# Two MLPs with the up-projection turned round: weights held, 256 tokens streamed, and the second norm applied to the sum

## The reference, cut to what matters

```
h2 = rms_norm(x, norm2_w) * (1 + scale2) + shift2
x  = x + gate2 * (square(relu(h2 @ w_ff1)) @ w_ff2)          # first MLP

h  = rms_norm_2(x, norm_mlp_g)
x  = x + square(relu(h @ mlp_w_in)) @ mlp_w_out              # second MLP
```

## Time and profile before

| | |
|---|---|
| median of the runs | 2431.68 us |
| the two runs | 2431.48 and 2431.89 us |
| span of the profiled execution | 2431.4 us |
| PE busy | 2359.0 us (97%) |
| VectorE busy | 1594.6 us (66%) |
| ScalarE busy | 1039.6 us (43%) |

### The profile page before, as it was taken

How to read it: one execution, slowest core, us unless ns; L and a number is a source line. 1 busy time by engine, 2 the same in 40 slices (tenths; PEclk the granted TensorE clock), 3 DMA queues, 4 the chain that set the end, 5 groups by cost and what they waited for, 6 DMA issues and landing times.

```text
span 2431.4 us, 27934 instructions
## 1 busy us (share of the span) xinstructions
PE 2359.0 (97%) x10954; PEld 1968.0 (81%) x10954; DVE 1594.6 (66%) x1284; ACT 1039.6 (43%) x890; POOL 51.4 (2%) x56
## 2 busy tenths in 40 slices
PE   4899999999999999999999999999999999999999
PEld 3777888887888888888887888878888888888887
DVE  7868989987666666655568456556555565565554
ACT  2245553435333333333334556664443433433432
POOL 1011000001000000000000000000000000000000
PEclk9789999999999999999999999999999999999999
DMA  9988987755676776655554545444555655555552
GB/s 355 362 300 311 361 311 268 252 199 169 231 241 231 234 242 224 224 190 181 183 190 171 177 160 168 156 138 158 183 191 183 191 184 192 189 188 190 190 189 104
DMA packets 235129, 520.30 MB, mean 214 GB/s; under 512 B 9705, under 2 KB 10162, under 8 KB 232370
## 3 DMA queue, kind: packets, MB, share of 16 engines
q1 hardware_dynamic: 234352, 519.15, 63.2%
q10 hardware_dynamic: 706, 0.17, 0.0%
HBM read 517.19 MB, written 2.10 MB: 214 GB/s over the span
## 4 chain that ended last, share of the span: by engine, by line
PE 90%; DVE 4%; DMA 2%; ACT 2%; issue 1%; DVEq 1%; POOL 1%; ACTq 0%; SPq 0%
PE PS L257 28%; PE PS L259 28%; PE PS L258 28%; DMA ada_raw<-in_w_ada_dram 2%; PE PS L1695 2%; PE PS L1734 1%; PE PS L1669 1%; DVE w_lo L247 1%; PE PS L306 1%; ACT w_hi L243 1%; POOL rstd L609 1%; PE PS L1679 1%; DVE ada_acc L1144 0%; DVEq L1511 0%; PE PS L1799 0%
## 5 line engine op out<-in xcount | busy, mean ns | idle before, releaser
L247 DVE TENSOR_TENSOR w_lo<-raw,w_hi 128x2048 fp32r<-128x2048 f32 x392 | 897.6, 2291 | 688.4 <-ACT w_hi L243 683.4
L243 ACT ACTIVATE w_hi<-raw 128x2048 fp32r<-128x2048 f32 x392 | 750.9, 1916 | 1149.1 <-PE PS L259 1137.7
L257 PE MATMUL PS<-w_hi,A_hi 128*128 128x512 f32 x2112 | 839.7, 398 | 10.0 <-DVE A_lo L361 3.5
L259 PE MATMUL PS<-w_hi,A_lo 128*128 128x512 f32 x2112 | 827.5, 392 | 0.0
L258 PE MATMUL PS<-w_lo,A_hi 128*128 128x512 f32 x2112 | 827.2, 392 | 0.0
L257 PEld LDWEIGHTS PS<-w_hi,A_hi 128*128 128x128 f32 x2112 | 400.6, 190 | 92.2 <-ACT qT L738 2.8
L259 PEld LDWEIGHTS PS<-w_hi,A_lo 128*128 128x128 f32 x2112 | 399.5, 189 | 84.9
L258 PEld LDWEIGHTS PS<-w_lo,A_hi 128*128 128x128 f32 x2112 | 400.4, 190 | 81.2 <-issue 1.0
L257 PE MATMUL PS<-w_hi,H_hi 128*128 128x512 f32 x1024 | 401.6, 392 | 2.0 <-issue 1.3
L259 PE MATMUL PS<-w_hi,H_lo 128*128 128x512 f32 x1024 | 398.9, 390 | 0.0
L258 PE MATMUL PS<-w_lo,H_hi 128*128 128x512 f32 x1024 | 398.5, 389 | 0.0
(11 more groups left out here) (267 smaller groups left out, 1108.0 us busy)
## 6 DMA issues: line engine op xcount, KB each, us to landing
raw<-in_w_ff_dram SPq DMA_DIRECT2D x128, 1024.0 KB, 5.3
raw<-in_mlp_w_in_dram SPq DMA_DIRECT2D x64, 1024.0 KB, 5.4
raw<-in_mlp_w_out_dram SPq DMA_DIRECT2D x64, 1024.0 KB, 5.0
raw<-in_w_in_dram SPq DMA_DIRECT2D x56, 1024.0 KB, 8.1
X<-in_w_ada_dram SPq DMA_DIRECT2D x96, 512.0 KB, 5.7
raw<-in_sb_w_qkv_dram SPq DMA_DIRECT2D x48, 1024.0 KB, 5.1
ada_raw<-in_w_ada_dram SPq DMA_DIRECT2D x32, 1024.0 KB, 9.8
raw<-in_w_out_dram SPq DMA_DIRECT2D x16, 1024.0 KB, 6.6
```

The source lines that it names most:

```text
L243: act.activation(w_hi[:, j, :, :], raw[:, j, :, :], ACT.Copy).then_inc(hi_rdy, 1)
L247: dve.tensor_tensor(w_lo[:, j, :, :], raw[:, j, :, :], w_hi[:, j, :, :].bitcast(F32), ALU.subtract).then_inc(lo_rdy, 1)
L257: pe.matmul(bank(pair + t), h, w_hi[:, j, k, :], start=first, stop=False)
L259: mm = pe.matmul(bank(pair + t), l, w_hi[:, j, k, :], start=False, stop=last)
```

## The change

- PE: all up-projections but the first unit of the first MLP use the new `up_chunk`. It holds 128 x 128 blocks of the weights (`w_hi`, `w_lo`) as the stationary operand and streams the 256 tokens of `A_hi` or `A_lo`. A chunk has 4 column blocks x 4 k tiles x 3 = 48 matmuls of 256 columns. The result has hidden features on partitions and tokens along the row, four pieces of 256 in two banks.
- The turn is gone for these units: ScalarE makes relu into `RE` and, after a drain, `Square` of `RE` straight into `H_hi`; VectorE squares `RE` into `SQ` and makes `H_lo` as `SQ - H_hi` (`rest`). The first unit of the first MLP keeps its turn.
- The next up on PE waits for `relu_rdy` instead of `sq_rdy`.
- Second MLP: relu has no scale and doesn't wait for the norm. The sum is gathered in `ACC` (its first down copies, `fresh`), `row_r` is `rstd` squared, and after the loop VectorE adds `ACC * row_r` to `X` in eight steps of 512 columns; the last down block is added in two such steps per quarter, with the same factor.

```diff
+        def up_chunk(pe, B, j, pair):
+            pe.wait_ge(lo_rdy, 4 * B + j + 1)
+            for c in range(CH):
+                out = bank(pair + c // 2, S * (c % 2), S * (c % 2) + S)
+                cols = slice(P * c, P * c + P)
+                for k in range(CH):
+                    h, l = A_hi[:, CH * j + k, :], A_lo[:, CH * j + k, :]
+                    first = j == 0 and k == 0 and c % 2 == 0
+                    last = j == CH - 1 and k == CH - 1 and c % 2 == 1
+                    pe.matmul(out, w_hi[:, j, k, cols], h, start=first, stop=False)
+                    pe.matmul(out, w_hi[:, j, k, cols], l, start=False, stop=False)
+                    mm = pe.matmul(out, w_lo[:, j, k, cols], h, start=False, stop=last)
+            mm.then_inc(chunk_done, 1)
...
 # ScalarE
-                def relu(B, U, pair):
+                def relu(B, U, pair, par):
                     act.wait_ge(chunk_done, 4 * (B + 1))
                     if not isinstance(U, int) or U:
                         act.wait_ge(sq_rdy, U)
-                    if m == 0:
-                        act.activation(RE[:, :, :], PS[:, pair:pair + 2, :], ACT.Relu).then_inc(relu_rdy, 1)
-                    else:
-                        for t in range(T):
-                            ins = act.activation(RE[:, t, :], bank(pair + t), ACT.Relu, scale=rstd[:, t:t + 1])
-                        ins.then_inc(relu_rdy, 1)
...
+                        if not isinstance(U, int) or U > 1:
+                            act.wait_ge(h_hi, U)
+                    act.activation(RE[:, :, :], PS[:, pair:pair + 2, :], ACT.Relu).then_inc(relu_rdy, 1)
+                    if par is not None:
+                        act.drain()
+                        act.activation(H_hi[:, par, :, :].rearrange("p k s -> p (k s)"), REf, ACT.Square).then_inc(h_hi, 1)
...
 # VectorE
-                    other = RE[:, :, :] if m else PS[:, pair:pair + 2, :]
-                    dve.tensor_tensor(SQ[:, :, :], other, RE[:, :, :], ALU.mult).then_inc(sq_rdy, 1)
+                        dve.wait_ge(h_lo, U)
+                    dve.tensor_tensor(SQ[:, :, :], RE[:, :, :], RE[:, :, :], ALU.mult).then_inc(sq_rdy, 1)
...
+                        if fresh:
+                            dve.wait_ge(chunk_done, 4 * B + j + 1)
+                            dve.tensor_copy(ac, PS[:, b:b + 2, :]).then_inc(acc_read, 1)
...
+                    d()
+                    for b in range(4):
+                        for t in range(T):
+                            xs = X[:, t, NC_ * b:NC_ * (b + 1)]
+                            dve.scalar_tensor_tensor(out=xs, in0=ACC[:, t, NC_ * b:NC_ * (b + 1)], scalar=row_r[:, t:t + 1], in1=xs,
+                                                     op0=ALU.mult, op1=ALU.add)
+                    d()
...
-                dve.tensor_tensor(X[:, :, cols], X[:, :, cols], PS[:, pb:pb + 2, :], ALU.add).then_inc(acc_read, 1)
+                for t in range(T):
+                    ins = dve.scalar_tensor_tensor(out=X[:, t, cols], in0=bank(pb + t), scalar=row_r[:, t:t + 1], in1=X[:, t, cols],
+                                                   op0=ALU.mult, op1=ALU.add)
+                ins.then_inc(acc_read, 1)
...
 # PE
                     if turned is None and not turn_last:
-                        pe.wait_ge(sq_rdy, U)
+                        pe.wait_ge(relu_rdy, U)
                     for j in range(CH):
-                        a_chunk(pe, B, j, pair, turned)
+                        if turned is not None:
+                            pe.wait_ge(a_lo, KT // 2 * turned + 2 * (j + 1))
+                        up_chunk(pe, B, j, pair)
...
-                        if j == 1 and turn_next:
-                            turn_unit(U + 1)
```

More of the change, by code:

```diff
@@ L859, in up @@
+                    act.activation(RE[:, :, :], PS[:, pair:pair + 2, :], ACT.Relu).then_inc(relu_rdy, 1)
+                    if par is not None:
+                        act.drain()
+                        act.activation(H_hi[:, par, :, :].rearrange("p k s -> p (k s)"), REf, ACT.Square).then_inc(h_hi, 1)
+                def up(B, U, par):
                     for j in range(CH):
                         split_hi(act, B + 1, j)
[L861 to L866, removed]
@@ L868, in down @@
-                def down(B, U, par, end=False):
+                    relu(B, U, 0, par)
+                def down(B):
                     for j in range(CH):
[L870 to L873, removed]
+                        split_hi(act, B + 1, j)
                 for j in range(CH):
                     split_hi(act, M + 1, j)
-                if m:
-                    act.wait_ge(rstd_rdy, POWER_OF[5])
@@ L879, in mlp @@
-                relu(M, NU * m, pairs[2])
+                relu(M, NU * m, pairs[2], 0 if m else None)
                 for j in range(CH):
                     split_hi(act, M + 2, j)
[L882 to L885, removed]
+                    if m == 0 and j == 1:
+                        act.wait_ge(h_tr, 1)
+                        act.activation(H_hi[:, 0, :, :].rearrange("p k s -> p (k s)"), PS[:, 6:8, :], ACT.Copy).then_inc(h_hi, 1)
@@ L886, in mlp @@
+                relu(M + 1, NU * m + 1, 0, 1)
+                down(M + 2)
                 with act.Fori(0, NU // 2 - 1) as i:
                     for e in range(2):
-                        up(M + 3 + 4 * i + 2 * e, NU * m + 2 + 2 * i + e)
-                        down(M + 4 + 4 * i + 2 * e, NU * m + 1 + 2 * i + e, e)
+                        up(M + 3 + 4 * i + 2 * e, NU * m + 2 + 2 * i + e, e)
+                        down(M + 4 + 4 * i + 2 * e)
             act.wait_ge(g_rdy, 5)
@@ L1461, in rows_half, with mlp, square @@
                 d()
-            def mlp(m, M, total):
-                def square(U, pair):
+            def mlp(m, M):
+                def square(U):
                     dve.wait_ge(relu_rdy, U + 1)
+                    if isinstance(U, int) and U == 1:
+                        dve.wait_ge(h_tr, 1)
                     if not isinstance(U, int) or U:
-                        dve.wait_ge(h_tr, U)
-                    other = RE[:, :, :] if m else PS[:, pair:pair + 2, :]
-                    dve.tensor_tensor(SQ[:, :, :], other, RE[:, :, :], ALU.mult).then_inc(sq_rdy, 1)
+                        dve.wait_ge(h_lo, U)
+                    dve.tensor_tensor(SQ[:, :, :], RE[:, :, :], RE[:, :, :], ALU.mult).then_inc(sq_rdy, 1)
                 def gate_sum(pair, half):
@@ L1484, in up, with rest @@
                             gate_sum(pair, 0)
-                    square(U, 0)
-                def turn(U, par):
+                    square(U)
+                def rest(U, par, turned=False):
                     dve.wait_ge(h_hi, U + 1)
-                    flat = "p k s -> p (k s)"
-                    dve.tensor_tensor(H_lo[:, par, :, :].rearrange(flat), PS[:, 6:8, :],
-                                      H_hi[:, par, :, :].rearrange(flat).bitcast(F32), ALU.subtract).then_inc(h_lo, 1)
+                    dve.wait_ge(sq_rdy, U + 1)
+                    src = PS[:, 6:8, :] if turned else SQ[:, :, :]
+                    dve.tensor_tensor(H_lo[:, par, :, :].rearrange("p k s -> p (k s)"), src.rearrange("p a n -> p (a n)"),
+                                      H_hi[:, par, :, :].rearrange("p k s -> p (k s)").bitcast(F32),
+                                      ALU.subtract).then_inc(h_lo, 1)
                 def gates(n):
@@ L1499, in gates, with down @@
                         dve.tensor_tensor(gate_w[:, 1, cols], bank(6 + b % 2), gate_w[:, 0, cols], ALU.add).then_inc(gate_rdy, 1)
-                def down(B, U, par, pair=None, into=None):
+                def down(B, U, par, pair=None, into=None, fresh=False):
                     for j in range(CH):
                         split_lo(dve, B + 1, j)
-                        ac = total[:, :, NC_ * j:NC_ * (j + 1)]
+                        ac = ACC[:, :, NC_ * j:NC_ * (j + 1)]
                         b = pairs[1 + j % 2]
-                        dve.tensor_tensor(ac, ac, PS[:, b:b + 2, :], ALU.add).then_inc(acc_read, 1)
+                        if fresh:
+                            dve.wait_ge(chunk_done, 4 * B + j + 1)
+                            dve.tensor_copy(ac, PS[:, b:b + 2, :]).then_inc(acc_read, 1)
+                        else:
+                            dve.tensor_tensor(ac, ac, PS[:, b:b + 2, :], ALU.add).then_inc(acc_read, 1)
                         if j == 1 and par is not None:
-                            turn(U + 1, par)
+                            rest(U + 1, par)
                         if into is not None:
@@ L1519, in mlp @@
                     split_lo(dve, M + 1, j)
-                square(NU * m, pairs[2])
+                square(NU * m)
+                if m:
+                    rest(NU * m, 0)
                 for j in range(CH):
                     split_lo(dve, M + 2, j)
[L1523 to L1527, removed]
+                    if m == 0 and j == 1:
```

(20 more changed lines are left out.)

2 lines of the change are left out of this document (1 added, 1 removed).

## The result

The changed kernel takes 2463.6 us (2462.72 and 2464.48) against 2431.68: ratio 1.013, 95% interval 1.010 to 1.0159. That is 32 us slower, where I had forecast 21.8 us less. The difference is under the 2% that the prediction put for "no change", but its interval is clear of 1. The profiled execution is the one of 2462.72 us, with a span of 2461.0, 29.6 us above the span before. The time lies at the upper end of my range, but on the other side of the kernel before: of my cases the first rival came true, in which each matmul carries its own overhead, and on top came two waits in the MLPs for which I had put nothing.

The account below looks back on a forecast made before the run. PE was taken to bound the kernel by its matmul pace. Turns -27.3, up-projections +3.8 and the end +1.5 and +0.2 summed to -21.8 us, giving about 2410 us, with a range from 2390 to 2464.

Parts of the forecast that it names:

- the first rival: Up-projections: overhead is each matmul's own, 120.1 ns per 256-column matmul, in all +14.5 us, so 2446; chance 0.33.
- What bounds the kernel: Whole kernel: nearly all time is PE's own pace, PE being busy for 97% of the span.
- The up-projections, p = 114: 5952 matmuls of 256 columns at 114 ns each in place of 2976 at 226.7: +3.8 us.
- I lean to the columns: Up-projections: the 13.4 ns overhead of a 512-column matmul belongs to its columns, giving 113.4 ns at 256.
- Load and stream share one way in: Slower rival in the up-projections: weight load and stream pass one port, 136 ns a matmul, so 2541 us; chance 0.10.
- The turns, -27.3: Between up and down of a unit on PE: 30 removed turns at 0.91 us each save 27.3 us.
- the paragraph on waits: PE's and VectorE's waits in the loops: the renamed waits and the weight queue cost 0.
- PE's next up waits for relu in place of the square; both ended a whole down earlier. 0: Start of each up on PE: the renamed wait costs 0.
- VectorE and ScalarE in the loops, the table: Loops: VectorE has the same count and sizes, ScalarE stays below half busy even with two possible 1.28 us table loads; 0.
- The end of the first MLP: Last loop block: VectorE's gate work holds the chain, so PE would only wait longer and that turn saves nothing.
- The end, +1.7: Last down: VectorE's eight steps hold back PE's third chunk, +1.5 us, and the last quarter takes +0.2.
- Range and sign: Whole kernel: 21.8 us less than before, range 2390 to 2464 us, chance of falling within it 0.83.

Follow-up runs that it names:

- the pace run: Separate kernel without the computation, PE alone running back-to-back matmuls: fp32r with 128-column weights 226.67 ns at 512 columns, 120.0 at 256; plain f32 at 256 took 215.8.
- the one-transpose runs: Kernel before, seven of eight transposes left out of every turn but the first unit's: 2417.4 us; also with VectorE's addition ahead of its split: 2409.4 us.

## Why the prediction was wrong, step by step

- **What bounds the kernel**: right. PE in every account above.
- **The up-projections, p = 114**: this term was mis-sized, and with it the forecast fell. It measured 120.0, so +39.6 and not +3.8 us. The step that failed is "I lean to the columns". One pace, 226.7 at 512 columns, can't tell an overhead of each matmul from one of its columns; I had written both down, 120.1 and 113.4, and chose by an argument on the lower clock that, as I said there, fitted both. The f32 row at 111.7 made 114 look near, but it is a pace of another format, for which the pace run has 2.5 ns over the stream where fp32r has 13.3. The pace runs settle it. The first rival's price, 2446, less the 1.7 us of the end, is what the kernel takes once its waits are gone: 2444.5.
- **Load and stream share one way in**: its 136 ns is refuted by the 120.0. The load isn't innocent either: its width changes the pace, in a way that I can't put into a rule.
- **The turns, -27.3**: the size was right, as the one-transpose runs show (-23 for seven of the eight transposes), but it wasn't free to take. The failed step is in the paragraph on waits: I asked what the turn cost on PE and not which wait ended behind it. The trace before had it: an addition ends about 5.6 us after its own chunk's 24 matmuls, the chunk between takes 5.44, and then came 0.91 us of turn. +10.7 us. The prediction let PE wait in the loops only for `H_lo` or a weight chunk, and otherwise kept all terms but p within 5 us; the wait was for `acc_read`.
- **"PE's next up waits for relu in place of the square; both ended a whole down earlier. 0"**: right in the loops, wrong for the second up of the second MLP, which has no down ahead and no shared bank. Before, it had no such wait at all. +3.1 us, and +2.3 for the clock that fell behind the stall.
- **VectorE and ScalarE in the loops, the table**: right. `Square` of 1063 ns stands for the copy of 1008, and no table is loaded in either MLP.
- **The end of the first MLP**: VectorE's chain bounds it still, as said.
- **The end, +1.7**: right, 1.6.
- **Range and sign**: the rival's price plus 16 us of waits gave 2463.6. The range held it, at its edge, by luck: for waits that I hadn't priced. The sign was wrong.

## What to carry to other kernels

Where the overhead belongs to each matmul, as with 128-column weights here, halving the stream doubles what it costs in all. Whose it is is found by timing the format at two lengths; one length can't tell. When work is taken off the bounding engine, list each semaphore that it waits for behind that work, and ask when each is signalled: a wait of the same length may have been hidden there. When a wait is renamed, go through its first and last use by hand, since loops hide them.

## What the runs showed of the hardware

- An fp32r matmul with 128-column weights has a pace of N / 2.4 + 13.33 ns at 256 to 512 columns; bf16 and plain f32 have about 2.5 in place of 13.3. At the lower clock fp32r has none: 213.3 ns at 256 columns.
- The pace depends on what alternates. 512 and 256 columns in turn take 353.2 ns a pair, grouped about 348, and streams of one kind 346.7. Behind a switch from 256 the first five matmuls of 512 run at 228 to 236, and behind a turn's transposes, in the kernel before, up to nine do at 224 to 236.
- fp32r with 64-column weights and 128 columns streamed reaches 60 ns; with 128-column weights the load holds it at 111.6.
- Behind a stall of 3.25 us PE's granted clock was at its lower level for 5.7 us, which cost 2.3 us more.
